# Splitting two weight units between the gate functions and squaring the keys behind the root: a two-layer mixer on one Trainium2 core

## The reference, cut to what matters

```python
h = rms_norm(x, norm_mix[0])
u, gate, xq = split(h @ w_in_a)                       # 512 columns each
u = causal_conv4(u) + conv_b                          # four taps
r, i = sigmoid(blocks(u) @ w_r + b_r), sigmoid(blocks(u) @ w_i + b_i)
log_a = -8 * r * softplus(-lam)
a, b = exp(log_a), sqrt(-expm1(2 * log_a)) * (i * u)
y_mix = scan(a, b) * gelu(gate)                       # hs[t] = a[t] * hs[t-1] + b[t]

kv = rms_norm(mem, g_mem) @ w_kv                      # 256 memory rows
k, v = split(kv)                                      # 4 heads of 128
q, k = rms_norm(xq heads, q_gain), rms_norm(k heads, k_gain)
y_mem = softmax(q @ k.T / sqrt(128)) @ v
x = x + concat(y_mix, y_mem) @ w_out[0]
```

## Time and profile before

| What | Value |
|---|---|
| median of 3 runs | 1320.63 us (1318.27 to 1322.15) |
| the profiled execution | 1321.03 us |
| its span, first to last instruction | 1319.2 us |
| mean granted TensorE clock | 0.997 |
| PE busy | 1293.1 us, 98% |
| DVE busy | 875.3 us, 66% |
| ACT busy | 707.1 us, 54% |
| POOL busy | 109.4 us, 8% |
| read from HBM | 222.16 MB, 169 GB/s over the span |

### The profile page before, as it was taken

One profiled execution on the slowest core, in us unless ns is written; L12 is line 12 of the kernel. 1 busy time (PEld: TensorE's weight loads), 2 busy tenths in 40 slices (PEclk: granted clock), 3 DMA queues, 4 the chain that ended last, 5 costly groups with the idle time before them and its releaser, 6 DMA issues.

```text
span 1319.2 us, 18605 instructions
## 1 busy us (share of the span) xinstructions
PE 1293.1 (98%) x7253; PEld 1118.4 (85%) x7253; DVE 875.3 (66%) x1185; ACT 707.1 (54%) x1182; POOL 109.4 (8%) x112
## 2 busy tenths in 40 slices
PE   6989999999999999999999999999999999999998
PEld 5868888888888888888998888888889988888887
DVE  5866666667635756566886766666677766766665
ACT  6774544446565545455654555555465545555553
POOL 1102000003200300001011030000021010100000
PEclk9999999999999999999999999999999999999999
DMA  9435655556422564645732255555556323556561
GB/s 365 166 113 159 240 175 207 176 179 215 166 96 96 193 215 167 213 171 176 256 131 69 74 178 187 190 187 190 176 192 224 112 80 96 176 191 190 190 187 42
DMA packets 62327, 224.43 MB, mean 170 GB/s; under 512 B 7192, under 2 KB 7328, under 8 KB 62240
## 3 DMA queue, kind: packets, MB, share of 16 engines
q1 hardware_dynamic: 59616, 214.23, 48.8%
q0 software_dynamic: 1904, 6.82, 1.6%
q10 hardware_dynamic: 720, 2.19, 0.4%
HBM read 222.16 MB, written 1.05 MB: 169 GB/s over the span
## 4 chain that ended last, share of the span: by engine, by line
PE 91%; DVE 4%; ACT 3%; issue 1%; POOL 0%; DMA 0%; ACTq 0%; DVEq 0%; POOLq 0%
PE ps L345 18%; PE ps L292 17%; PE ps L297 17%; PE ps L296 17%; PE ps L353 8%; PE ps L455 4%; PE ps L490 2%; PE ps L513 2%; PE ps L821 2%; PE ps L343 1%; DVE wlo L1584 1%; ACT whi L1008 1%; ACT scr L1063 1%; DVE small L1669 0%; PE ps L494 0%
## 5 line engine op out<-in xcount | busy, mean ns | idle before, releaser
L1584 DVE TENSOR_TENSOR wlo<-raw,whi 128x1024 fp32r<-128x1024 f32 (+1 forms) x402 | 479.4, 1213 | 240.9 <-ACT whi L1008 238.9
L1008 ACT ACTIVATE whi<-raw 128x1024 fp32r<-128x1024 f32 (+1 forms) x409 | 422.1, 1048 | 273.9 <-PE ps L345 173.2
L345 PE MATMUL ps<-XT,whi 128*128 128x512 f32 x1024 | 279.4, 394 | 0.0
L345 PEld LDWEIGHTS ps<-XT,whi 128*128 128x128 f32 x1024 | 177.2, 189 | 25.4
L292 PE MATMUL ps<-whi,HT_hi 128*128 128x512 f32 (+1 forms) x512 | 193.7, 378 | 0.5 <-DVE HT_lo L1773 0.5
L296 PE MATMUL ps<-wlo,HT_hi 128*128 128x512 f32 (+1 forms) x512 | 192.4, 376 | 0.0
L297 PE MATMUL ps<-whi,HT_lo 128*128 128x512 f32 (+1 forms) x512 | 192.3, 376 | 0.0
L353 PEld LDWEIGHTS ps<-XT,wlo 128*128 128x128 f32 x896 | 137.4, 189 | 18.9
L353 PE MATMUL ps<-XT,wlo 128*128 128x256 f32 x896 | 142.5, 281 | 0.0
L292 PE MATMUL ps<-whi,XT 128*128 128x512 f32 (+1 forms) x304 | 120.6, 397 | 3.3 <-DVE XT L1801 2.3
L297 PE MATMUL ps<-whi,XT 128*128 128x512 f32 (+1 forms) x304 | 116.8, 384 | 0.0
(11 more groups left out here) (258 smaller groups left out, 1700.3 us busy)
## 6 DMA issues: line engine op xcount, KB each, us to landing
raw<-in_w_m SPq DMA_DIRECT2D x152, 512.0 KB, 4.2
raw<-in_w_n SPq DMA_DIRECT2D x108, 512.0 KB, 4.2
raw<-in_w_c SPq DMA_DIRECT2D x48, 512.0 KB, 4.3
raw<-in_w_o SPq DMA_DIRECT2D x32, 512.0 KB, 3.5
raw<-in_w_kv SPq DMA_DIRECT2D x16, 512.0 KB, 4.2
raw<-in_w_b SPq DMA_DIRECT2D x16, 512.0 KB, 4.3
raw<-in_w_w SPq DMA_DIRECT2D x16, 512.0 KB, 4.9
raw<-in_w_a SPq DMA_DIRECT2D x12, 512.0 KB, 7.9
```

Of the source, the lines that this page charges most:

```text
L345: m = pe.matmul(outs[f][:, :], hi[:, j, at(f)], both, start=(k == 0), stop=(k == KT - 1))
L1008: act.activation(whi[:, g % NSPLIT, 0:w], raw[:, g % NRAW, 0:w], ACT.Copy).then_inc(split_hi, 1)
L1584: dve.tensor_tensor(wlo[:, g % NSPLIT, 0:w], raw[:, g % NRAW, 0:w], whi[:, g % NSPLIT, 0:w].bitcast(F32), ALU.subtract).then_inc(split_lo, 1)
```

## The change

Seven edits, all in the first layer:

- The second tile of memory rows is transposed into banks 0 and 1 in place of 6 and 7.
- PE runs the values' last unit differently: three units of `mv0`, the transposes of the keys, half of unit 19, the first scores, the other half.
- The first unit of the output projection moves from behind the transposes of round 2 to ahead of those of round 1, the second from behind the transposes of round 3 to ahead of them.
- ACT splits unit 16 ahead of the four `Tanh` and unit 17 between `Tanh` and `Exp`, unit 18 ahead of the root.
- ACT squares the keys directly behind the root, ahead of the load of the exponential's table, and splits unit 19 behind that.
- DVE splits units 16 and 17 ahead of the product for the root and 18 ahead of the root's result; it sums the squares ahead of the scan, and splits unit 19 behind it.
- DVE signals `conv` ahead of the split of unit 13, and makes `HT_lo` (event `ylo`) behind the first largest score.

```diff
-            def turn_norm(k, tt):
+            def turn_norm(k, tt, first=6):
...
-                    turn(f"n{k}.{tt}.{h}", 6 + h, [xn[:, tt, (4 * h + j) * P:(4 * h + j + 1) * P] for j in range(4)])
+                    turn(f"n{k}.{tt}.{h}", first + h, [xn[:, tt, (4 * h + j) * P:(4 * h + j + 1) * P] for j in range(4)])
...
-            feature_pairs("u", (2, 3), [a["w_a"][u] for u in range(4)], {2: lambda: turn_norm(1, 0), 3: lambda: turn_norm(1, 1)})
+            feature_pairs("u", (2, 3), [a["w_a"][u] for u in range(4)], {2: lambda: turn_norm(1, 0), 3: lambda: turn_norm(1, 1, 0)})
...
-            mem_kv(0, "mv", [2, 3], {2: lambda: mem_keys(0)})
+            mem_values = by_tile(["mv0.0", "mv0.1"], (2, 3), [a["w_kv0"][4 + u] for u in range(4)], tok(MX))
+            for _ in range(6):
+                next(mem_values)
+            mem_keys(0)
+            next(mem_values)
             mem_ready(0, 2)
...
-            attend(["ma0"], {"ma0": mem_spec(0)}, {1: lambda: mem_ready(0), (2, 2): lambda: (pe.wait_ge(ev("ylo"), 1), next(out_left)),
-                                                   (3, 2): lambda: next(out_left)})
+            attend(["ma0"], {"ma0": mem_spec(0)}, {1: lambda: mem_ready(0), (1, 1): lambda: (pe.wait_ge(ev("ylo"), 1), next(out_left)),
+                                                   (3, 1): lambda: next(out_left)},
+                   first=lambda: next(mem_values))
...
-            for dst, fn, c in ((11, ACT.Tanh, "lh"), (7, ACT.Exp, "lc")):
+            for n, (dst, fn, c) in enumerate(((11, ACT.Tanh, "lh"), (7, ACT.Exp, "lc"))):
+
+                splits(fills["mk0.0"].pos + 1 + n)
...
-            splits(fills["mk0.0"].pos + 1)
+            splits(fills["mk0.0"].pos + 3)
             act.wait_ge(ev("b2"), 1)
             act.activation(slot(8, 1024), slot(8, 1024), ACT.Sqrt, scale=-0.25).then_inc(ev("bsq"), 1)
+            for tt in range(TT):
+                act.wait_ge(bank_full[fills[f"mk0.{tt}"].bank], fills[f"mk0.{tt}"].turn)
+                act.activation(hrow[:, tt, :], PS[fills[f"mk0.{tt}"].bank][:, :], ACT.Square).then_inc(ev("sqf"), 1)
 
             act.activation(sm("z4", 4), sm("z4", 4), ACT.Exp)
-            splits(fills["mk0.0"].pos + 2)
-            rows_in("mk0", hrow[:, :, :].rearrange("p a b -> p (a b)"), None)
+            splits(fills["mk0.0"].pos + 4)
...
-                splits(fills["u.1"].pos + AHEAD + s - 1)
+                if s < 3:
+                    splits(fills["u.1"].pos + AHEAD + s - 1)
             dve.memset(sm("one", 1), 1.0).then_inc(ev("conv"), 1)
+            splits(fills["u.1"].pos + AHEAD + 2)
...
+            splits(fills["mk0.0"].pos + 2)
             dve.wait_ge(ev("decay2"), 1)
             dve.tensor_tensor(s8, om, th, ALU.mult).then_inc(ev("b2"), 1)
-            splits(fills["mk0.0"].pos)
+            splits(fills["mk0.0"].pos + 3)
             dve.wait_ge(ev("bsq"), 1)
             step(dve.tensor_tensor(uc, uc, s8, ALU.mult))
+            fox_sums(2, sm("rk8", 8), hq(8, P).rearrange("p n d -> p (n d)"), P)
             for f in range(4):
-                if f < 3:
-                    splits(fills["mk0.0"].pos + f)
...
-            fox_sums(2, sm("rk8", 8), hq(8, P).rearrange("p n d -> p (n d)"), P)
-            splits(fills["mk0.1"].pos + AHEAD)
-            splits(fills["mv0.1"].pos)
...
+            splits(fills["mv0.1"].pos)
             gelu()
-            rglru_lo()
-            soft(["ma0"], {1: second_gains, 3: lambda: rows_out(["ma0"], "ma0", 0, xn[:, 0, 512:1024])}, True)
+            soft(["ma0"], {0: rglru_lo, 1: second_gains, 3: lambda: rows_out(["ma0"], "ma0", 0, xn[:, 0, 512:1024])}, True)
```

## The result

The changed kernel takes 1313.28 us in the median of 5 runs (1311.1 to 1314.85), against 1320.63 us before (5 runs, 1318.27 to 1323.69). The ratio is 0.9941 with a 95% interval of 0.9928 to 0.9953: 7.4 us less, where 5.9 were forecast. A second set of 5 runs gave 1314.12 us, ratio 0.9948 (0.9936 to 0.9961). The profiled execution has a span of 1313.0 us, against 1319.2.

A forecast was written before the change was run, and what follows sets the result against it. PE, busy 98% of the span, was taken as the bound. Its waits and slow stretch in the first layer fall from 9.79 to 3.85 us, gain 5.94, from 1321.03 to 1315.1; given as 1315.0, range 1312.4 to 1318.4.

The forecast's parts named there:

- Other banks: Second tile's transposes on PE no longer wait for banks 6 and 7; the gate's units start 1.67 us sooner.
- The signal: DVE's `conv` ahead of unit 13's split costs and brings nothing; cover left 1.4 us, or 0.3 without it.
- Splits between the functions: ACT and DVE split units 16 and 17 early, so PE need not wait before the values; 4.42 us removed.
- the pause of 2.80 and the slow stretch: PE's stand between keys and values, 2.80 us, and nine matmuls behind at the lower clock, 1.62; both go.
- Squares behind the root: Keys' squares on ACT directly behind the root; DVE starts their sum at 70.53 against 75.43, 4.90 us sooner.
- from there everything is the same as before: Behind the sum of squares, mean, power and scaled keys keep their order and times; scaled keys start at 74.62.
- PE's own order: Reordered values, scores and output units on PE leave waits of 0.75, 1.8, 0.3 and 1.0 us.
- M: Distance on PE from the first tile's memory-row transposes to the first transpose of output rows; 68.32 us before.
- The clock did not fall: Rival: PE's new pauses between 76.1 and 80.8 lower the clock and the 1.62 us return; 1316.7, chance 0.13.
- The chain of the keys was not late: Rival: keys' chain 1 to 2.5 us later than worked out, PE waiting in full; 1316 to 1317.6, chance 0.12.
- the slower case: Rival: root waits for DVE's product, which must slip 8 us to cancel the gain; 1323 us, chance 0.03.
- The lead was not given back: Rival: a later wait on something not shifted, such as a DMA, takes the gain; 1320.6 us, chance 0.07.

The follow-up runs named there:

- splits only: Kernel before, with only units 16 to 19 split as in the changed kernel: 1321.29 us, ratio 1.0005 to before.
- squares back: Changed kernel, with the keys' squares again behind the second table load and unit 19, their sum behind the scan: 1316.47 us, ratio 0.9968 to before.
- unit 19 beside it: Changed kernel, ACT copying unit 19 ahead of the root and DVE making its rest beside POOL's power: 1314.67 us, ratio 0.9957 to before.
- one square more: Changed kernel, with one more square of the decay on ACT ahead of the root: 1314.78 us, ratio 0.9960 to before.
- banks only: Kernel before, with only the second tile of memory rows moved to banks 0 and 1: 1318.96 us, ratio 0.9992 to before.
- Old PE order: Changed kernel, with PE's previous order of values, scores and output projection: 1315.07 us, ratio 0.9959 to before.
- late copies: Changed kernel, with ACT copying units 20 to 23 later, by a cap on copying ahead: 1310.78 us, ratio 0.9925 to before.

## Why the prediction was right

**Other banks, 1.67: right.** The gate's units start at once, and the single edit measured 1.66 and 1.63. The small gain on DVE came too: its second piece of the memory rows starts at 44.02 - 0.79 = 43.23, as forecast, where it started at 43.50 before, and the taps end at 50.48 + 2.02 - 0.79 = 51.71, against 52.00: 0.3 sooner, forecast 0.2.

**The signal: right**, nothing in either direction.

**Splits between the functions: right with its limit.** The forecast said that the pause of 2.80 and the slow stretch go, and that the chain of the keys comes next. The splits alone show how hard that limit is: 4.4 us removed, 4.0 given back, 3.54 of them in one wait at the keys' transposes. The sum counted 4.42 for this edit; alone it is worth 0.4. What it is worth beside the other edits is not measured, since no run takes only the splits back out of the changed kernel. Taken back one by one, squares (4.5), banks (1.6) and PE's order (1.6) already make 7.7, more than the 6.75 of all together, so the shares overlap and can't be added up.

**Squares behind the root: right in mechanism.** Reckoned from the same start (0.79 off), the sum of squares begins at 71.25 - 0.79 = 70.46, forecast 70.53. The table loads take 1.28 and the root starts 0.02 behind, so the drain that the Trainium skill adds (ScalarE: Activation LUTs, What ACT_TABLE_LOAD costs) does not show on this path; by it the sum would have come at 71.9. **The mis-sized term is the step "from there everything is the same as before"**: POOL's power took 1.96 in place of 2.55, and the scaled keys start at 74.75 - 0.79 = 73.96, forecast 74.62.

**PE's own order: right, one wait too long.** Waits were forecast as 0.75, 1.8, 0.3 and 1.0, 3.85 in all; they are 0.2, 1.9, 0.5 and 0.6, 3.2 in all. The first is short because of the power, 0.59 faster; the last since in round 2 the copy of the transposed rows came sooner: PE goes on at 92.79 - 0.79 = 92.00, forecast 92.45. By the sum's own terms the gain is 9.79 - 3.2 = 6.6, forecast 5.94, and the power makes up nearly all of the difference; the errors of the last two waits, +0.2 and -0.4, partly cancel, which is luck. M was forecast as 98.6 - 36.49 = 62.1, and is 61.57.

**The rivals.** The clock did not fall in the changed kernel's pauses: the three that stand between 76.8 and 85.7 together make 2.6. It fell in the versions that stand longer there (squares back, near 79.4; splits only, near 89.8). The chain of the keys was not late: no copy of a unit on ACT had to wait for PE between the gates' functions and the root, and the root starts at 68.90 - 0.79 = 68.11, forecast 66.89 + 1.28 = 68.17. DVE's product for it ends at 65.72 + 1.23 - 0.79 = 66.16, forecast 66.2, so the slower case was far. The lead was not given back. What the median gained beyond the forecast (7.4 against 5.9) is 0.8 from M and for the rest within the spread of the runs: the second comparison gave 6.6. The inner bounds of the forecast, 1313.1 to 1316.2, were not taken from one base: gains of 4.8 to 7.5 around the centre of 1315.0 make 1313.4 to 1316.1. The median of 1313.28 lies at their lower end, inside the range that was given (1312.4 to 1318.4).

## What to carry to other kernels

A wait that is removed is worth what the next wait on the same path leaves of it; here removing 4.4 us of stall and slow clock was worth 0.4 alone, while the chain behind stayed as it was, so list the next limit before pricing an edit, and look beyond the neighbouring wait. When an engine far from busy (ACT at 54%) feeds the bound engine, its work on stock (copies made ahead) belongs behind what is wanted now: a cap on how far it runs ahead gave 2.8 us more for a few lines. In a kernel of 1.3 ms, a local distance on the bound engine resolves 0.1 us where the times resolve 2.

## What the runs showed of the hardware

**POOL's power takes longer when DVE is inside an instruction as it starts.** The same instruction on 128 x 8 numbers took 2.55 to 2.58 us in each case in which DVE had just begun a weight's rest, and 1.96 (once 1.95) where it had just begun the scan. In the table it is the power of the keys:

| Kernel | DVE as it starts and behind | Power, us |
|---|---|---|
| before | two rests | 2.55 |
| changed, squares back | one rest, then gelu | 2.55 |
| changed, unit 19 beside it | one rest, then scan | 2.56 |
| changed | scan | 1.96 |
| changed, one square more | scan | 1.96 |

Neither is its time alone. Later in the changed kernel DVE is idle during the whole power (POOL's row at 738.12), and in another layer DVE begins a subtraction with two inputs in SBUF, the kind that makes `HT_lo`, 0.04 behind the power's start (DVE's row at 627.72):

```profile
738.12 1.66 POOL L1452 TENSOR_TENSOR small<-small,powc 128x8 f32<-128x8 f32 x1 [33.54 <-DVE small L1663]
```

```profile
627.68 1.68 POOL L1452 TENSOR_TENSOR small<-small,powc 128x8 f32<-128x8 f32 x1 [16.02 <-DVE small L1663]
```

```profile
627.72 1.44 DVE L2022 TENSOR_TENSOR HT_lo<-xn,HT_hi 128x1216 fp32r<-128x1216 f32 x1
```

All fourteen profiles agree: 1.64 to 1.66 with DVE idle as the power starts, 1.68 in this case. So the opcode does not order the cases; what is under way does. In the version with unit 19 beside the power, the rest ends at 71.37 + 1.22 = 72.59, 1.06 behind the power's start, and the power takes 0.90 more than alone. In the changed kernel the first of the four scans ends at 72.58 + 0.68 = 73.26, 0.51 behind the start, and the power takes 0.30 more. What follows on DVE adds nothing: one rest costs as much as two. This fits a POOL that stands until DVE's running instruction is nearly over; no run was made to test it.

The Trainium skill (GPSIMD Engine Reference, Specifications) says that POOL shares its SBUF interfaces with VectorE and that they collide when a DVE instruction reads two inputs from SBUF. The rest and the scan both do, and both cost time, in agreement; the subtraction that began behind the power did not slow it, and of that the section says nothing.

**One pause does not tell whether the clock falls.** The granted clock is 0.50 behind a pause of 2.64 in the kernel before, and again with banks only. With splits only it held 1.00 behind a pause of 3.54, and fell some 8 us later, after another of 2.07. The windows of splits only, columns as above:

```profile
82.00:84.00 2.00, 2.00 (x12) 1.72 (x11) 0.00 (x0) 2.00 (x4) 0.00 (x0) 1.00 0.00 0
...
90.00:92.00 2.00, 1.76 (x6) 1.21 (x5) 1.71 (x9) 2.00 (x6) 0.00 (x0) 0.50 0.78 248
```

With squares back, a pause of the same 3.54 was followed by the lower clock at once. Far behind, PE stands 0.5 us at the same instruction four times in the run. In the kernel before the clock fell to 0.50 behind one of these:

```profile
1042.99 1.97 PE L821 MATMUL ps<-scr 128*128 128x64 f32 x16 [0.51 <-DVE scr L2075]
```

```profile
1046.00:1048.00 2.00, 2.00 (x7) 1.64 (x7) 1.93 (x6) 0.00 (x0) 0.00 (x0) 0.50 0.54 217
```

In the changed kernel the same pause, at 1038.44, was followed by 1.00:

```profile
1040.00:1042.00 2.00, 2.00 (x17) 1.92 (x16) 1.56 (x3) 0.00 (x0) 0.00 (x0) 1.00 0.59 160
```

Old PE order, late copies and one square more have such a fall behind a pause of 0.51 as well (near 688, 684 and 1038), and the other ten profiles none, so it belongs to the execution and not to the change. So the length of a single pause orders these cases badly; I count the price (1.6 us behind the pause of before) as a chance and not as a certainty.
